# Squares of relu made on ScalarE instead of VectorE in the feed-forward stage of a one-core decoder block

## The reference, cut to what matters

```
hf = rms_norm(x, norm_ff_pre)
ff = jnp.square(jax.nn.relu(hf @ w_ff_in)) @ w_ff_out      # 1024 -> 4096 -> 1024
return x + rms_norm(ff, norm_ff_post)
```

## Time and profile before

| | us |
|---|---|
| median of 3 runs | 785.5 (785.39 to 787.23) |
| profiled execution, its own time | 785.12 |
| its span in the profile | 783.4 |
| TensorE busy | 765.7 (98%) |
| VectorE busy | 529.3 (68%) |
| ScalarE busy | 365.2 (47%) |

### The profile page before, as it was taken

How to read it: one execution, slowest core, us unless ns; L and a number is a source line. 1 busy time by engine, 2 the same in 40 slices (tenths; PEclk the granted TensorE clock), 3 DMA queues, 4 the chain that set the end, 5 groups by cost and what they waited for, 6 DMA issues and landing times.

```text
span 783.4 us, 9921 instructions
## 1 busy us (share of the span) xinstructions
PE 765.7 (98%) x3640; PEld 640.7 (82%) x3640; DVE 529.3 (68%) x883; ACT 365.2 (47%) x609; POOL 58.4 (7%) x110
## 2 busy tenths in 40 slices
PE   7999999999999999999999999999999999999994
PEld 6888888888887888888888998888887888878873
DVE  5624667677777336885635779746895579667897
ACT  4522656666565744232325545544443444334542
POOL 3000000022223003000001200000000000000002
PEclk9999999999999999999999999999999999999998
DMA  8333232212132532326331452136003620262002
GB/s 295 109 114 101 70 92 79 83 55 82 55 83 80 188 101 61 114 75 242 107 108 54 161 186 57 54 139 211 27 3 104 259 65 1 56 240 81 0 1 108
DMA packets 91581, 80.29 MB, mean 102 GB/s; under 512 B 2833, under 2 KB 77585, under 8 KB 91537
## 3 DMA queue, kind: packets, MB, share of 16 engines
q1 hardware_dynamic: 90864, 79.70, 31.5%
q10 hardware_dynamic: 672, 0.01, 0.0%
HBM read 77.60 MB, written 2.10 MB: 102 GB/s over the span
## 4 chain that ended last, share of the span: by engine, by line
PE 90%; DVE 6%; ACT 1%; DMA 1%; issue 0%; SPq 0%; POOL 0%; DVEq 0%; POOLq 0%; ACTq 0%
PE acc L1382 26%; PE acc L1384 26%; PE acc L1383 26%; DVE w_lo L1213 2%; PE aux L1383 1%; PE aux L1384 1%; PE aux L1382 1%; DVE sum L1236 1%; DMA w_raw<-in_w_in 1%; PE aux L1569 1%; PE aux L1495 1%; PE aux L1494 1%; PE aux L1504 1%; PE acc L1523 1%; PE acc L1520 1%; PE aux L1477 1%
## 5 line engine op out<-in xcount | busy, mean ns | idle before, releaser
L1382 PE MATMUL acc<-actB_hi,w_hi 128*128 128x512 f32 (+1 forms) x544 | 207.3, 381 | 0.8 <-DVE sum L1318 0.8
L1384 PE MATMUL acc<-actB_hi,w_lo 128*128 128x512 f32 (+1 forms) x544 | 205.4, 378 | 0.0
L1383 PE MATMUL acc<-actB_lo,w_hi 128*128 128x512 f32 (+1 forms) x544 | 205.2, 377 | 0.0
L931 DVE TENSOR_TENSOR w_lo<-w_raw,w_hi 128x1024 fp32r<-128x1024 f32 x72 | 87.8, 1223 | 83.9 <-ACT w_hi L648 83.1
L1382 PEld LDWEIGHTS acc<-actB_hi,w_hi 128*128 128x128 f32 x544 | 102.5, 188 | 19.6 <-DVE w_lo L1209 1.6
L1384 PEld LDWEIGHTS acc<-actB_hi,w_lo 128*128 128x128 f32 x544 | 102.4, 188 | 18.9
L1383 PEld LDWEIGHTS acc<-actB_lo,w_hi 128*128 128x128 f32 x544 | 102.5, 188 | 18.1
L648 ACT ACTIVATE w_hi<-w_raw 128x1024 fp32r<-128x1024 f32 x72 | 75.4, 1052 | 71.1 <-PE acc L1384 68.8
L1382 PE MATMUL acc<-w_hi,actB_hi 128*128 128x512 f32 x160 | 62.7, 392 | 1.5 <-DVE actB_lo L941 1.3
L1384 PE MATMUL acc<-w_hi,op_lo 128*128 128x512 f32 x160 | 63.5, 397 | 0.0
L1383 PE MATMUL acc<-w_lo,op_hi 128*128 128x512 f32 x160 | 63.4, 396 | 0.0
(11 more groups left out here) (192 smaller groups left out, 1292.1 us busy)
## 6 DMA issues: line engine op xcount, KB each, us to landing
w_raw<-in_w_in SPq DMA_DIRECT2D x44, 512.0 KB, 3.9
w_raw<-in_w_ff_in SPq DMA_DIRECT2D x32, 512.0 KB, 4.0
down_raw<-in_w_ff_out SPq DMA_DIRECT2D x16, 1024.0 KB, 6.9
w_raw<-in_w_b SPq DMA_DIRECT2D x8, 512.0 KB, 3.6
w_raw<-in_w_a SPq DMA_DIRECT2D x8, 512.0 KB, 3.5
w_raw<-in_w_o SPq DMA_DIRECT2D x8, 512.0 KB, 3.8
x<-in_x SPq DMA_DIRECT2D x4, 512.0 KB, 7.5
x<-in_x SPq DMA_DIRECT2D x1, 2048.0 KB, 9.0
```

Of the source, the lines that this page charges most:

```text
L931: nc.vector.tensor_tensor(w_lo[:, j], w_raw[:, j], w_hi[:, j].bitcast(F32), ALU.subtract).then_inc(lo_made, 1)
L1382: nc.tensor.matmul(o, a_hi, b_hi, start=first, stop=False)
L1383: nc.tensor.matmul(o, a_hi, b_lo, start=False, stop=False)
L1384: return nc.tensor.matmul(o, a_lo, b_hi, start=False, stop=last)
```

## The change

The 32 squares (128x512 each) move from VectorE to ScalarE, right behind the relu that they read, and before `hi_ahead`. ScalarE waits for its own relu (`relu_made`) first. VectorE's square and its wait for relu are gone; it still waits for `sq_made` behind `lo_ahead`. The wait ahead of the even unit's `s_raw` (that the previous pair's `s_raw` has been read) is set on `op_lo_made`, VectorE's own last low part, where it was on ScalarE's `op_hi_made`.

```diff
-                    nc.scalar.activation(ff_act[:, m % 4], acc[:, bank], ACT.Relu).then_inc(relu_made, 1)
+                    f = ff_act[:, m % 4]
+                    nc.scalar.activation(f, acc[:, bank], ACT.Relu).then_inc(relu_made, 1)
+                    act.wait_ge(relu_made, m + 1)
+                    nc.scalar.activation(f, f, ACT.Square).then_inc(sq_made, 1)
                     hi_ahead(item(c, n))
                     act.wait_ge(sq_made, m + 1)
...
                     f = ff_act[:, m % 4]
-                    dve.wait_ge(relu_made, m + 1)
-                    nc.vector.tensor_tensor(f, f, f, ALU.mult).then_inc(sq_made, 1)
                     lo_ahead(item(c, n))
                     dve.wait_ge(sq_made, m + 1)
                     if n % 2 == 0:
                         if m >= 2:
-                            dve.wait_ge(op_hi_made, 3 * (c * PAIRS + j))
+                            dve.wait_ge(op_lo_made, 3 * (c * PAIRS + j))
```

## The result

| | before | after |
|---|---|---|
| median, us | 785.49 (20 runs) | 786.89 (20 runs) |
| profiled execution: own time, span | 785.12, 783.4 | 787.32, 785.6 |
| first relu of the stage to last relu | 278.78 | 279.64 |
| last relu to the end of the span | 49.20 | 50.00 |
| VectorE busy, ScalarE busy | 529.3, 365.2 | 508.8, 382.7 |

The ratio of after to before is 1.002, with a 95% interval of 1.0014 to 1.0026: the kernel is 1.4 us slower. That is inside the 0.3% called no change ahead, but with 20 runs each it is told from zero: the interval is 1.1 to 2.0 us, which takes in the forecast sum of 1.46 and leaves out 0.66. Four of the 20 runs of either kernel took about 2 us more than the others (for the changed one the granted clock was 0.991 in them and 0.995 to 0.997 in the rest), and so did some runs of the experiments, which widens the intervals.

The account below looks back on a forecast made before the run. TensorE was taken as the bound, with VectorE full too at the end. The terms 0.40 + 0.40 + 0.66 = 1.46 us gave 786.58 from the profiled execution and 786.96 from the median, so 786.8 us; range 785.2 to 788.3.

Parts of the forecast that it names:

- What bounds: Whole kernel: TensorE busy 98% of the span, never waiting in the up units; freeing VectorE pays only where TensorE waits.
- The delay of a last unit: Last up unit: `w_hi` starts 1.16 us after relu's start in place of 0.50, so everything behind is 0.66 us later.
- the bounds, 0.56 and 1.15: Least and most delay x of `w_hi` in us, as no in-place square was in the trace; sums 1.16 and 2.9.
- Chunk 0: none: Last unit of chunk 0: `w_lo` starts about 0.2 us later, with no effect on TensorE.
- P6 in chunks 1 and 2: TensorE's weight load for P6 has 0.13 us of cover, comes 0.53 late, and TensorE loses 0.40 us in each chunk.
- The tail: Chunk 3 to the end: the end hangs on VectorE, whose run shifts by 0.66 us, and so does the end.
- The sum 3x - 0.52: Total loss in us for a `w_hi` delay x above 0.26, paid at three places; forecast 1.46.
- A: Rival: P1's adds come in time in chunks 1 and 2, so only the tail moves, +0.66, 785.8 to 786.2; chance 0.15.
- B: Rival: the square is dearer on ScalarE than its row says, sum 2.0, 787.1 to 787.5 us; chance 0.10.
- C: Rival: ScalarE's wait for relu plus square gets long in last units; slower past 0.3%, 788.0 to 788.4 us; chance 0.10.
- D: Rival: the freed 22 us of VectorE remove TensorE's waits, 2.1 us at most, 783.0 to 783.4; chance 0.05.
- the even unit's lateness: Even units: relu late by 0.37 us at most, `w_lo` by about 1 us; said not to pile up.

Follow-up runs that it names:

- experiment 1: Against the changed kernel, all 32 squares stay on ScalarE but stand behind the rounding of the next weight block (`hi_ahead`): 785.35 us beside 785.45 for the kernel before.
- experiment 2: Changed kernel, but ScalarE squares only the last up units of chunks 1 to 3, VectorE the other 29: 786.63 us beside 785.45 for the kernel before.
- experiment 3: Changed kernel, but ScalarE squares the first seven units of every chunk and VectorE the last one: 785.44 us beside 785.45 for the kernel before.
- experiment 5: Changed kernel, but ScalarE squares only the very last up unit, in chunk 3: 786.12 us beside 785.55 for the kernel before.
- experiment 4: Changed kernel plus one more in-place relu between relu and square in each chunk's last unit: 788.76 us beside 785.45 for the kernel before.
- experiment 7: On top of experiment 1, one weight sum (T3b) per chunk moved ahead of the last unit's `w_lo` on VectorE: 784.24 us beside 785.55 for the kernel before.
- experiment 8: On top of experiment 7, P2's first bank taken ahead of the `w_lo` block in chunks 1 and 2: 782.73 us beside 785.55 for the kernel before.

## Why the prediction was right

- **What bounds.** That TensorE never waits in the up units, and that freed VectorE time alone gains nothing, held: experiment 1 frees the same time and changes nothing, and VectorE's idle time ahead of `w_lo` just grows.
- **The delay of a last unit, 0.66 us.** Measured 0.67 from relu to `w_hi` and to `w_lo`. The parts: square 0.63 (0.635 in the median of 32), wait of ScalarE for itself 0.03. Of the bounds, 0.56 and 1.15, the nearest row was right, and the 0.09 seen behind the squares with a sum was not that of a plain wait.
- **Chunk 0: none.** `w_lo` comes 2.25 after relu in place of 2.05, the 0.2 forecast, and no wait appears there.
- **P6 in chunks 1 and 2, 0.40 us each.** Load late by 0.53; the matmuls lose 0.41. A has grown by 0.86 for 0.80. Experiments 2, 3 and 5 place it: with the squares of the last units of chunks 1 and 2 it comes, without them it doesn't.
- **The tail, 0.66 us.** VectorE's run shifted by 0.66 from relu to the merges (746.00 - 735.60 against 743.94 - 734.20). B has grown by 0.80, but up to the issue of the last store it is 0.66 (47.10 and 47.76 from relu). The other 0.14 lie behind that issue, 2.24 against 2.10, and experiment 1, which has no delay, has 2.20 there. So they are scatter and no part of the change.
- **The sum 3x - 0.52**, at a second point: x = 1.34 gives 3.5, measured 3.3 (experiment 4).
- **The time, 786.8.** The median is 786.89. The profiled execution was to take 786.58 and took 787.32; 0.54 of that miss is the drift ahead of the stage.
- **Rivals.** A (only the tail) falls to the two new waits of 0.58 and 0.57. B and C (a dearer square, a long wait) fall to 0.63 and 0.03 us; with B falls the page's rule for this case: of the Trainium skill's "ScalarE: Activation LUTs", "Rules for kernel authors", the estimate of 0.73 us stands against 0.635 measured, and VectorE's 0.688 is no cheaper. The prediction left out two conditions of that page: its preference for VectorE is argued from bf16 with a single source, and its 0.3 us is for a bias given as a pointer; the data here are float32. D (the freed time removes TensorE's waits) fell as the change stands. Its limit of 2.1 us was too low for what the schedule holds, since it counts only TensorE's waits and the tail is bound by VectorE: experiments 7 and 8 together give 2.8. And it put the two 0.8 us down to a `w_lo` that waits for ScalarE; experiment 8 shows that TensorE waited for the add behind it.
- **Not weighed enough:** the even unit's lateness. I had it as harmless since the weight sum ends before `w_hi`. That holds only while the last square is on ScalarE; experiment 3 shows 0.18 us of it.

## What to carry to other kernels

Moving an operation to a less busy engine can cost by its place in that engine's queue: here, ahead of what VectorE waited for, the square delayed it by its whole length, though ScalarE was idle half of the time, and behind it the square cost nothing. Look for the stretches in which the engines are coupled without slack (here the last unit before a change of stage), work out the cover there in hundredths, and count each of them; the average load tells nothing. Freed time gained nothing here by itself; it did when something from the critical run was moved into it.

## What the runs showed of the hardware

ScalarE waiting for its own relu went on 0.03 us after that had ended (569.33 to 569.36), no more than VectorE needed for the same signal before. It also loses the overlap: from start to start it is 0.63, where an independent operation follows relu by 0.50. A stall of TensorE is cheaper than the lateness of its weight load: 0.53 late cost 0.41, since behind a wait the first matmul follows its load by 0.04 (579.92 to 579.96) instead of 0.23, and the next one 0.30 behind it instead of 0.23.
